# A ring of gathered rows lengthened with buffers that other stages leave idle, in a two-layer diffusion block with product-key experts

## The reference

```
u = u_tab[idx]                                   # 16 rows of 1024 per head and token
a = gelu(einsum('chkd,cd->chk', u, xc))
w = softmax(scores) * a
out = einsum('chk,chkd->cd', w, v_tab[idx])      # 16 more rows of 1024
```

## Time and profile before

| | us |
|---|---|
| median of 3 runs | 2510.23 (2505.12 to 2511.02) |
| the profiled execution | 2506.35 |
| its span, first to last instruction | 2504.6 |
| PE busy | 1411.9 (56%) |
| DVE busy | 1533.9 (61%) |
| POOL busy | 1486.5 (59%) |
| DMA, mean over the span | 375 GB/s |

### The profile page before, as it was taken

The page is one execution under the profiler, slowest core; times in us unless marked ns, Lnnn a source line. Parts: engine busy times, 40 slices in busy tenths (PEclk is TensorE's granted clock), DMA queues, the critical chain, the costliest instruction groups (busy, mean ns, idle before and its releaser), DMA issues.

```text
span 2504.6 us, 22058 instructions
## 1 busy us (share of the span) xinstructions
PE 1411.9 (56%) x7198; PEld 639.6 (26%) x7198; DVE 1533.9 (61%) x3968; ACT 347.0 (14%) x697; POOL 1486.5 (59%) x1546
## 2 busy tenths in 40 slices
PE   7899574556665574354345444379866546433333
PEld 3448321123323341011011110026634124001000
DVE  1235877877955656766776554414779756687542
ACT  2331201112301111010001000014123011000000
POOL 0002766776776677776777667610376766677773
PEclk9899687678787786677756755679878778766566
DMA  9845999999999999999999999995799999999997
GB/s 347 323 157 204 388 406 407 409 409 370 392 406 409 405 407 407 409 409 407 409 403 409 403 406 409 380 344 174 271 407 381 405 408 405 409 408 409 410 410 265
DMA packets 287856, 939.02 MB, mean 375 GB/s; under 512 B 27760, under 2 KB 28544, under 8 KB 287488
## 3 DMA queue, kind: packets, MB, share of 16 engines
q0 software_dynamic: 221184, 805.40, 81.3%
q1 hardware_dynamic: 66560, 132.21, 14.4%
HBM read 936.46 MB, written 1.05 MB: 374 GB/s over the span
## 4 chain that ended last, share of the span: by engine, by line
DMA 29%; POOL 23%; PE 21%; DVE 14%; issue 10%; ACT 2%; SPq 1%; POOLq 0%; DVEq 0%; ACTq 0%
POOL RING L730 23%; DMA RING<-in_p_v,IDV 20%; DMA RING<-in_p_u,IDX 8%; PE acc L1300 6%; DVE RING L823 5%; PE wk L1501 4%; PE wk L1362 3%; PE wk L1486 2%; PE wk L1286 1%; PE wk L1329 1%; DVE TI L812 1%; PE wk L1339 1%; PE wk L1533 1%; DVE OHR L1076 1%; DVE OHR L1080 1%
## 5 line engine op out<-in xcount | busy, mean ns | idle before, releaser
L823 DVE SCALAR_TENSOR_TENSOR RING<-RING,acc 128x1024 f32<-128x1024 f32 x768 | 916.6, 1219 | 486.8 <-DMA RING<-in_p_u,IDX 444.4
L1300 PE MATMUL acc<-RING,ST 128*32 128x512 f32 x3072 | 608.2, 933 | 943.9 <-DMA RING<-in_p_v,IDV 941.8
L730 POOL DMA_INDIRECT RING<-in_p_u,IDX x768 | 740.6, 964 | 615.7 <-DVE WG L1091 344.5
L730 POOL DMA_INDIRECT RING<-in_p_v,IDV x768 | 744.3, 969 | 384.2 <-issue 205.8
L1300 PEld LDWEIGHTS acc<-RING,ST 128*32 128x32 f32 x3072 | 119.5, 146 | 1335.0 <-issue 1322.1
L1259 ACT ACTIVATE GA<-A 128x16 f32<-128x16 f32 x48 | 10.3, 215 | 735.9 <-DVE RING L823 735.9
L1501 PE MATMUL wk<-HT,WR 128*128 128x256 f32 (+1 forms) x576 | 106.8, 343 | 0.0
L1362 PE MATMUL wk<-WR,HT 128*128 128x512 f32 x224 | 101.1, 608 | 0.0
L1501 PEld LDWEIGHTS wk<-HT,WR 128*128 128x128 f32 x576 | 94.0, 193 | 17.0 <-issue 7.8
L1533 PE MATMUL wk<-SELW,WE 128*128 128x512 f32 x96 | 70.0, 818 | 24.6 <-DVE WE L844 24.6
L1261 ACT ACTIVATE ST<-wk 128x512 f32<-128x512 f32 x48 | 28.7, 597 | 370.0 <-PE wk L1533 370.0
(11 more groups left out here) (187 smaller groups left out, 1641.0 us busy)
## 6 DMA issues: line engine op xcount, KB each, us to landing
RING<-in_ada_w SPq DMA_DIRECT2D x27, 1024.0 KB, 12.9
WR<-in_ada_w SPq DMA_DIRECT2D x20, 1024.0 KB, 11.2
WR<-in_p_w_q SPq DMA_DIRECT2D x17, 1024.0 KB, 11.8
RING<-in_p_u,IDX POOLq DMA_INDIRECT x768, 11.8
RING<-in_p_v,IDV POOLq DMA_INDIRECT x768, 11.8
RING<-in_p_w_q SPq DMA_DIRECT2D x11, 1024.0 KB, 5.8
WR<-in_o_w_in SPq DMA_DIRECT2D x10, 1024.0 KB, 15.5
WR<-in_e_w_in SPq DMA_DIRECT2D x8, 1024.0 KB, 14.3
```

What stands on the lines that cost most here:

```text
L730: pool.indirect_dma_start(out=ring[:, n % NU, :], out_offset=None, in_=tables[table], in_offset=bass.IndirectOffsetOnAxis(ap=rows, axis=0) ...
L823: nc.vector.scalar_tensor_tensor(out=U[:, s % NU, :], in0=U[:, s % NU, :], scalar=1.0, in1=acc[:, 1, :], op0=ALU.mult, op1=ALU.mult, accum ...
L1300: ins = nc.tensor.matmul(acc[32 * g:32 * g + 32, 0, hf * 512:hf * 512 + 512], ST[:, c % 2, s, :], V[:, s % NV, hf * 512:hf * 512 + 512], s ...
```

## The change

The ring's buffers are no longer n mod 8. `gather_rows` walks the schedule and gives each gather the buffer used longest ago among the ring's eight of its kind and those borrowed at that step. `EXTRA` lists the borrowed ones: buffer, kind, first step and the step after the last (layer 1's steps count from L1 = 129; a buffer of HTC or half a slot of WR is one row). So u has 11 rows in steps 0 to 4, 8 from 5 to 44, 9 to 13 from 45 to 83, 14 and 15 from 84 to 100, then 12 and 11, and in layer 1 it has 9, from its step 20 on 10 and from 33 on 13. v has 9 at first, 11 or 12 in steps 6 to 26, 10 until 34, 12 until 74, 10, then 12 until 122, 10 at the end of layer 0 and until step 20 of layer 1, 13 from there and 16 from step 33. POOL waits at the first gather of a window for what used the buffer before (`opened`), and after that for the row that was in it. Whoever uses a buffer again waits for the last row that was lent (`emptied`): SP before slot 2 and XSLOT, ACT before some evictions, DVE before layer 1's first attention output. DVE and PE wait for a semaphore of each buffer instead of one of each ring place.

HT becomes two tiles, HTL and HTC, of the latent and the context tokens; XSLOT lies in HTC instead of X. In `block_slots`, blocks used from step 4 of layer 0's gathers on until its end take two slots of WR instead of three, and slot 2 is given again to the fourth block of layer 1's front. The order of instructions on PE, DVE and ACT stays the same but for the waits.

```
         if i < early:
             slot = i % (WSLOTS + len(EARLY_ROWS))
         else:
-            free = [*range(WSLOTS)] + [XSLOT] * (at >= end)
+            free = [*range(WSLOTS if last < sums[0] or at >= end else 2)] + [XSLOT] * (at >= end)
             free += EARLY_DOTS if last < dots[0] else ()
             free += EARLY_SUMS if last < sums[0] else ()
             free += RSLOTS[:4] if end <= at and last < dots[1] else ()
             free += RSLOTS[4:] if end <= at and last < sums[1] else ()
-            slot = min(free, key=lambda s: idle[s])
+            slot = min(free, key=lambda s: idle[s] if s != 2 or at < end else max(idle[s], (AT["experts_end", 0], -1)))
         idle[slot] = (last, i)
         u = users.setdefault(slot, [])
         slots.append((slot, len(u) + 1, u[-1] if u else None))
...
+EXTRA = [(("bc", 0), "u", 0, 5), (("bc", 1), "u", 0, 5), (("bc", 2), "u", 0, 5), (("h", 0), "v", 0, 22),
+         (("wr", 2, 0), "v", 6, 123), (("wr", 2, 1), "v", 6, 123), (("h", 3), "v", 8, 27),
+         (("htc", 0), "v", 35, 75), (("htc", 1), "v", 35, 75),
+         (("h", 1), "u", 45, 111), (("h", 0), "u", 50, 78), (("bc", 0), "u", 49, 101), (("bc", 1), "u", 49, 101), (("bc", 2), "u", 49, 101),
+         (("x", 2), "v", 78, L1 + 65), (("x", 3), "v", 78, L1 + 65), (("htc", 0), "u", 84, 127), (("htc", 1), "u", 84, 127),
+         (("h", 0), "u", 89, 128), (("h", 0), "u", L1, L1 + 65),
+         (("bc", 1), "v", L1 + 20, L1 + 65), (("bc", 2), "v", L1 + 20, L1 + 65), (("bc", 4), "v", L1 + 20, L1 + 65), (("h", 1), "u", L1 + 20, L1 + 65),
+         *[(("wr", s, a), "uv"[a], L1 + 33, L1 + 65) for s in range(WSLOTS) for a in range(2)]]
+
+
+def gather_rows():
+
+    rows, order, fills, used, last = {}, {}, {}, {}, {}
+    base = {"u": [("ring", i) for i in range(NU)], "v": [("ring", NU + i) for i in range(NV)]}
+
+    def place(kind, n, step):
+        now = [(r, -1) for r in base[kind]] + [(e[0], w) for w, e in enumerate(EXTRA) if e[1] == kind and e[2] <= step < e[3]]
+        row, w = min(now, key=lambda x: order.get(x, -1))
+        order[row, w] = len(rows)
+        fills[row] = fills.get(row, 0) + 1
+        rows[kind, n] = (row, fills[row], used.get((row, w), w))
+        used[row, w] = (kind, n)
+        last[w] = (kind, n)
+
+    for s in SCHEDULE:
+        if s[0] == "experts":
+            _, l, tile, h, q = s
+            c = chunk0(l, tile) + h
+            step = l * L1 + 4 * (c - 32 * l) + q
+            for i in range(4 * q, 4 * q + 4):
+                place("u", c * TOPK + i, step)
+            for i in range(4 * q, 4 * q + 4) if c > 32 * l else ():
+                place("v", (c - 1) * TOPK + i, step)
+        elif s[0] == "experts_end":
+            c = chunk0(s[1], ORDER[s[1]][-1]) + PH - 1
+            for i in range(TOPK):
+                place("v", c * TOPK + i, s[1] * L1 + 4 * (c + 1 - 32 * s[1]))
+    return rows, last
+
+
+ROWS, LAST_IN = gather_rows()
 
 
...
-        HT = sb("HT", [P, KC, 4 * P])
+        HTS = [sb(n, [P, KC, 2 * P]) for n in ("HTL", "HTC")]
...
 
         blk = {n: i for i, n in enumerate(BLOCKS)}
+
+        def row_at(row):
+
+            if row[0] == "ring":
+                return RING[:, row[1], :]
+            if row[0] == "wr":
+                return WR[:, row[1], 2 * row[2]:2 * row[2] + 2, :].rearrange("p k n -> p (k n)")
+            if row[0] == "htc":
+                return HTS[CTX][:, 4 * row[1]:4 * row[1] + 4, :].rearrange("p k n -> p (k n)")
+            return {"bc": BC, "h": H, "x": X}[row[0]][:, row[1], :]
+
+        def taken_out(kind, n):
+
+            return (dotted if kind == "u" else vsum), n + 1
+
+        def emptied(row, step):
+
+            return taken_out(*LAST_IN[next(w for w, e in enumerate(EXTRA) if e[0] == row and e[2] <= step < e[3])])
...
+                return HTS[CTX][:, :, :].rearrange("p k n -> p (k n)").rearrange("p (k n) -> p k n", k=KC // 2)
             r = EARLY_ROWS[slot - WSLOTS]
...
                 if before:
                     sp.wait_ge(*block_used(before))
+                    if slot == 2 and AT[before[:-1]] < AT["experts_end", 0] < AT[name[:-1]]:
+                        for a in range(2):
+                            sp.wait_ge(*emptied(("wr", 2, a), 6))
                 elif slot in RSLOTS[:4]:
                     sp.wait_ge(dotted, 32 * TOPK)
                 elif slot in RSLOTS:
                     sp.wait_ge(vsum, 32 * TOPK)
                 elif slot == XSLOT:
-                    sp.wait_ge(normed.sem, normed.at(1, 1, 3))
+                    for a in range(2):
+                        sp.wait_ge(*emptied(("htc", a), 84))
...
+            given = set()
+
+            def opened(w):
+
+                (what, *which), first = EXTRA[w][0], EXTRA[w][2]
+                if what == "bc":
+                    if first == 0:
+                        return evac(("out", 0, (2, 3), 1)) if which[0] == 0 else evac(("tqk", 0, 3, "q", 1))
+                    return evac(("out", 0, (0, 1), 1)) if first < L1 else made(("attC", 1, LAT, 15))
+                if what == "h" and which[0] == 0:
+                    return (made(("keys",)) if first == 0 else made(("out", 0, (0, 1), 1)) if first == 50 else
+                            evac(("tqk", 1, 3, "k", 0)) if first == 89 else made(("out", 1, (0,), 1)))
+                if what == "h" and which[0] == 1:
+                    return made(("attA", 0, LAT, 11)) if first < L1 else made(("attA", 1, LAT, 15))
+                if what == "h":
+                    return evac(("hT", 0, 1, (0, 1), 3))
+                if what == "htc":
+                    return made(("xin", 0, 3)) if first == 35 else made(("in", 1, 2, (2, 3)))
+                if what == "x":
+                    return normed.sem, normed.at(1, 1, 3)
+                return block_used([b for b, s in zip(BLOCKS, SLOTS) if s[0] == which[0] and
+                                   (first > L1 or AT[b[:-1]] < AT["experts", 0, ORDER[0][0], 1, 0])][-1])
+
+            def gather(kind, n, rows):
+                row, _, before = ROWS[kind, n]
+                if row[0] == "ring" and (n // 512, row) not in given:
+                    given.add((n // 512, row))
+                    users = [b for b, x in zip(BLOCKS, SLOTS) if x[0] == row_slot(n // 512, row[1])]
+                    if users:
+                        pool.wait_ge(*block_used(users[-1]))
+                if before != -1:
+                    pool.wait_ge(*(taken_out(*before) if isinstance(before, tuple) else opened(before)))
+                pool.indirect_dma_start(out=row_at(row), out_offset=None, in_=tables[kind],
+                                        in_offset=bass.IndirectOffsetOnAxis(ap=rows, axis=0)).then_inc(row_in[row], 16)
 
             def gather_u(c, s):
...
-                    dve.wait_ge(u_in[s % NU], 16 * (2 * c + s // NU + 1))
-                    nc.vector.scalar_tensor_tensor(out=U[:, s % NU, :], in0=U[:, s % NU, :], scalar=1.0,
+                    row, fills, _ = ROWS["u", c * TOPK + s]
+                    dve.wait_ge(row_in[row], 16 * fills)
+                    nc.vector.scalar_tensor_tensor(out=row_at(row), in0=row_at(row), scalar=1.0,
...
+                    if s == ("in", 1, 2, (2, 3)):
+                        act.wait_ge(*emptied(("h", 0), 50))
+                    elif (c, tiles[0]) == (2, 0):
+                        for a in range(3):
+                            act.wait_ge(*emptied(("bc", a), 49 * l))
...
-                for s in range(4 * q, 4 * q + 4):
-                    pe.wait_ge(v_in[s % NV], 16 * (2 * c + s // NV + 1))
+                rows = [ROWS["v", c * TOPK + s] for s in range(4 * q, 4 * q + 4)]
+                for row, fills, _ in rows:
+                    pe.wait_ge(row_in[row], 16 * fills)
...
```

52 lines of the change are left out of this document (23 added, 29 removed).

## The result

The changed kernel takes 2495.82 us, the median of 5 runs (2493.43 to 2499.97), against 2510.23 for the kernel before beside it (5 runs): a ratio of 0.995, 95% interval 0.9939 to 0.9962. That is 14.4 us less by the medians and 12.5 by the ratio, where 26 were forecast; it lies inside the range (2469 to 2502), but the gain is about half of the forecast's. The profiled execution took 2493.43, with a span of 2491.6 where before had 2504.6.

What follows compares the result with a forecast made beforehand. The 16 DMA engines' ceiling of about 409 GB/s was taken as the bound, so only their idle time could be regained: 9.5 + 5 + 2.5 + 3 + 3 + 0.5 = 23.5 us, forecast 2484 us, range 2469 to 2502.

Steps and rivals of the forecast that it cites:

- Part 3: Layer 0's start: eleven u rows instead of 8 in steps 0 to 4 gain 2.5 us, bounds 0 and 3.3.
- Part 6: Two weight slots under layer 0's gathers: loads land just in time or late but covered; 0 us, bounds 0 and -6.
- Part 1: Layer 1's tail: v ring from 8 to 16 rows lets gathers follow one another; gain 9.5 us, bounds 7 and 10.8.
- Part 2: Layer 0's tail: four weight loads leave later, into a stretch with room, and two v rows more; 5 us, bounds 0 and 9.
- Part 4: Layer 0's attention under the gathers, 570 to 700 us: waits behind PE go; gain 3 us, bounds 1 and 7.
- part 5: Layer 1's attention, 1900 to 1970 us: more v and u rows gain 3 us, bounds 1 and 4.4.
- small rest: The remaining shortfall of 700 to 1600 us gives 0.5 us, bounds 0 and 1.
- tails only: Rival, chance 0.16: gaps within phases are DVE's, moved loads eat layer 0's tail's free time; 10.5 us gained, 2496.

Runs made afterwards that it cites:

- late-opening kernel: The kernel before with v borrowing eight rows (16 in all) only from layer 1's step 60 on, u untouched: 2502.35 us, ratio 0.997.

## Why the prediction was right or wrong

The direction and the bound held: the engines' bytes don't change, the gain is idle DMA time, and layer 1's tail is the greatest term. The size and the rest of the order did not: the sum was 23.5 and the same steps measured 11.8 in the changed kernel's trace, and the second largest term brought nothing. That the time lies inside the range is no merit of the sum.

**Part 3, 2.5 forecast, 3.4 measured.** Right. 75.7 us became 72.3 (72.2 and 72.3 in the three other kernels with these rows, 75.9 and 76.6 in the two without). The feared gap where the ring shrinks did appear (260 to 300 us, 367 GB/s against 409 before), and 32-128 was not longer for it (276.4, 276.3). On the slow chips the start gains nothing.

**Part 6, nothing forecast, nothing measured.** The number I gave for it was weak: the 11.7 us of a lone load were set against 16 rows in the queue, 20.5 us, where by my own count some nine are in flight, 9 x 1.28 + 2.56 = 14.1. The changed kernel's trace says it better: the load sent at 1587.89 landed after 11.6 us while rows issued beside it took 21 to 27. The Trainium skill's rule of arbitration (DMA: Bandwidth & Descriptors, Queues, rings and completion order) agrees with this.

**Part 1, 9.5 forecast, 6.8 measured** (8.4 to 8.5 in five executions of four kernels with the same rows open, 7.5 by the ratio of the late-opening kernel alone). The mechanism was right; the stretch ran at 410 GB/s, though POOL still waited for PE. Missized was the allowance for the end: "the last rows pay some latency again" was put at 1.3 us, 10.8 less 9.5. The last row's way took 12.65 us instead of 5.86, 6.8 more, in which 16 engines' work becomes one engine's.

**Part 2, +5 forecast, -0.9 measured** (dots 256 to 512, before 830.0, after 830.9). This is the step that failed: "the same bytes come back in a stretch with 10.8 us to spare". I read the mean of 338 GB/s over 1600 to 1662 as room for other bytes wherever they came. But until 1620 that stretch was full, and the moved loads, sent at 1588, had landed by 1622. So what the dots had gained by dot 448 (8.3 us of the 10.2 forecast) was paid back before dot 511 (9.5), and only the hole behind it moved. The forecast even had the loads leave some 20 us ahead of the last dot, and didn't ask what the engines did in these 20 us. The lower end I gave, 0, was "if the v rows only lost their share to the loads"; u rows lost theirs too. Two more v rows brought nothing either (40.1 us from dot 511 to the last v sum with eight, 40.4 with ten). Whether loads sent after the last dot, or a v ring of sixteen there, would use the room was not tested. The Trainium skill's round robin by packets (same page and section), which I used only for loads that wait behind rows, says the same of rows beside loads; the rise of a v row's landing to 26.9 us agrees.

**Part 4, 3 forecast, 1.2 measured; part 5, 3 forecast, 1.3 measured** (layer 1's 512-767; the kernel with the late tail, which is the kernel before up to there, reads 681.5 where before reads 680.7; and 128-256 reads 363.7 and 365.2 in the two kernels that lend no row there, against 363.2 to 365.1 in those that do). So no gain is shown in either part. Both stretches rose in GB/s by what was forecast, 382 to 394 and 383 to 405, that is 3.8 us less short in each by the prediction's formula for the earlier trace rows. But what a fixed window shows is not what a fixed piece of work gains: the work in the window had shifted with everything before it. I had summed windows; the ledger by dots should have been the measure of the forecast as well.

Of the 11.7 us between 23.5 and 11.8, part 2 makes 5.9, part 1 2.7, part 4 1.8, part 5 1.7 and its small rest 0.5; part 3 gives 0.9 back. Of the rivals, "tails only" (2496) has the right number and most of the reasons: the loads ate what layer 0's tail had free, and the gaps within the phases gave little. It lacks the 3.4 of layer 0's start, and so has the number in part by luck.

## What to carry to other kernels

The mean rate of a stretch doesn't say where in it the engines are idle. Before moving transfers into such a stretch, cut it finer and set the holes beside the time at which the transfers will leave: these four left where the engines were full, took their time from the gathers beside them, and the idle time turned up at the drain. Look for a gain by fixed work (the n-th dot), not by fixed windows. Where the engines are full, more ring buys only the fill at the start and the drain at the end. And try a longer ring on more than one chip.
